# A decoder step on one core: the sample tokens' expert layer computed in the prologue, between the pieces of token tile 0's mixer

## The chip, the cores and the metric

One core of one Trainium2 chip runs the kernel. The metric is the device time in microseconds (us), lower is better. Most executions of a kernel agree within 0.3%.

## The reference

One layer of a hybrid decoder runs on 1024 prompt tokens and on 8 sample tokens, width 1024, in float32. Each token goes through a mixer (retention and dilated attention side by side) and then through PEER, a layer of product-key experts:

```python
qh = (xb @ w_pq).reshape(128, 8, 2, 64)             # 8 heads, two half queries
sc = einsum('thcq,hckq->thck', qh, sub_keys)        # 2 x 128 key scores a head
s1, i1 = top_k(sc[:, :, 0], 16); s2, i2 = top_k(sc[:, :, 1], 16)
# the best 16 of the 16 x 16 sums give 16 of the 16384 experts
g = softmax(top_s)
a = gelu(einsum('thkd,td->thk', peer_u[eidx], xb))
y = einsum('thk,thkd->td', g * a, peer_v[eidx])     # then x = x + gt2 * y
```

So each token reads 8 x 16 = 128 rows of `peer_u` and `peer_v`, 8 KB for the pair.

## The kernel before

Three blocks follow each other. `condition` makes the modulation rows. `decode` runs the sample's mixer and leaves its key scores in `sc_s`, its normed rows in the DRAM tensor `h2` and its mixed rows in `x_mid`. `layer`, from 262 us on, runs the prompt in T = 8 token tiles of 128. This document is about `layer`.

**The expert loop.** For each tile and head (N = 64 pairs, `n`) and each of 8 groups of two slots (`q`), POOL gathers one row of `uv` (u and v joined, 8 KB) for each of the 128 tokens: one indirect DMA of 1 MB a slot, into a ring of 8 buffers (`RING`). DVE takes the dot product with h2 (L1627), ACT makes Gelu, multiplies by the gate and scales the v half (L1107 to L1114), PE transposes and sums it in PSUM (`psA`, L1339) and then frees the two buffers (`s_free`), on which POOL's next two gathers wait. DVE chooses the experts of `n + 2` in the same groups (`choose`, parts 1 to 7).

**The mixer of each tile** is cut into pieces: on each engine a generator `front()` yields a due time and `Pace` runs the pieces between the loop's groups. Tile 0's pieces are all due at -1, so all of them run before the loop, in the order in which they are written: this is the prologue. Its order on PE: turn x, seven projections of four chunks (`product`, L1138), retention and attention of eight heads, turn of the mixed rows, output projection (2 products, w_out), turn of h2, queries (2 products, w_pq), turn of the queries; then `peer_scores` for the first three `n`. A projection's product writes one of two halves of `psS`, which DVE or ACT must have read before the next but one starts. DVE's evictions stand at `mark_read(t, j)`, its masking of the retention scores at L1443, the addition to x at L1544, the norm behind it at L1547 to L1554; ACT's square root of that variance is L1070.

**SP's queue** loads constants, then weight chunks of 512 KB into NB = 4 buffers `w`, each when PE has used the chunk four before it (`s_wu`), and the rows and stores of each tile.

**The sample's expert layer** has 8 tokens, whose 8 x 128 slots are turned: one gather a token, 128 experts on the partitions. Before, DVE chooses in the groups of n = N - 2; the choice goes to DRAM and comes back transposed by 8 small DMAs (16 experts x 8 tokens each) into `expT_f`, the gates the same way into `gateT`; POOL gathers behind the last prompt gather; DVE takes the dots against `h2b` (h2's row of each token, spread over 128 partitions and loaded by SP into `kTva`, free since the last tile's attention); ACT makes Gelu, DVE multiplies by the gate into one column of `coef`, and PE sums `coef` times v in `psS` (L1355). Two DVE operations and a store of y_sample end the kernel.

## Time and profile before

| | us |
|---|---|
| median of three runs | 3507.4 (3506.52 to 3515.91) |
| the profiled execution | 3499.32 |
| its span | 3497.5 |
| `layer` starts | 262.8 |
| first prompt gather, last prompt gather | 418.8, 3447.6 |
| DVE, ACT, PE busy, share of the span | 64%, 58%, 72% |

A busy share is a mean over the prologue, the loop and the tail, whose limits differ. In a timeline row stand the start in us, the length, the engine and the line, the operation, what it writes and reads, and the number of merged instructions (x16). In a windows row stand the stretch, its length, busy time and instructions of PE, PEld, DVE, ACT and POOL, the granted TensorE clock, the DMA share and GB/s. PE's float32 matmuls are recorded twice each: a 512-column product of one token is four records.

### The profile page before, as it was taken

What the parts mean: (1) busy time and instruction counts of PE and PEld (TensorE: products, weight loads), DVE (VectorE), ACT (ScalarE), POOL (GpSimd) and SP (SyncE); (2) the same over time, 40 slices, a digit from 0 to 9 for tenths busy, and PEclk for the clock granted to TensorE, in tenths of its full rate; (3) what the DMA queues carried; (4) which work ended last, traced back from release to release, by engine and by line L of the source; (5) the groups of instructions that cost most, each with busy time, mean ns of one, the idle gap of its engine ahead of it and who ended that gap; (6) DMA issues with size and microseconds to landing.
All of it is one profiled execution on the core that took longest, in us unless ns stands there. A gap on an engine that the chain in (4) does not pass through costs nothing.

```text
span 3497.5 us, 35906 instructions
## 1 busy us (share of the span) xinstructions
PE 2510.3 (72%) x12243; PEld 1758.0 (50%) x12243; DVE 2250.2 (64%) x5362; ACT 2037.0 (58%) x3417; POOL 1193.1 (34%) x1054
## 2 busy tenths in 40 slices
PE   8878587778767677688776776787776866565555
PEld 2224245445554565555654664555654655555553
DVE  0132366656676776666867876666976876776774
ACT  0101157655594776665766875665866766665663
POOL 0000023333342443333333433433333333444443
PEclk9988698889988888899787888899887888766777
DMA  8746599999999999999999999999999999999997
GB/s 311 260 152 203 196 373 381 392 374 414 414 401 396 390 394 413 406 415 415 408 413 406 387 393 413 405 415 416 411 406 406 384 396 403 421 420 413 414 419 316
DMA packets 272759, 1326.03 MB, mean 379 GB/s; under 512 B 36544, under 2 KB 37040, under 8 KB 139200
## 3 DMA queue, kind: packets, MB, share of 16 engines
q0 software_dynamic: 149072, 1083.68, 75.9%
q1 hardware_dynamic: 123504, 240.05, 19.0%
q8 instruction: 97, 1.59, 0.2%
q14 instruction: 86, 0.70, 0.0%
HBM read 1309.55 MB, written 14.09 MB: 378 GB/s over the span
## 4 chain that ended last, share of the span: by engine, by line
DMA 35%; PE 23%; ACT 16%; DVE 11%; issue 3%; POOL 3%; POOLq 0%; DVEq 0%; PEldq 0%; ACTq 0%
DMA pr_ring<-uv,pr_expert 25%; PE pairA L1339 11%; PE pairS L1138 9%; ACT pr_ring L1114 8%; DVE pr_ring L1627 6%; DMA sb_w<-w_out 4%; DMA sb_w<-w_pq 4%; POOL pr_ring L936 3%; ACT pr_act_h L1110 2%; ACT L1107 2%; PE bank L1138 2%; DMA sb_w<-w_in 1%; ACT L1060 1%; ACT pr_act_h L1107 1%; ACT pr_sp L1060 1%
## 5 line engine op out<-in xcount | busy, mean ns | idle before, releaser
L936 POOL DMA_INDIRECT pr_ring<-uv,pr_expert x1024 | 1170.0, 1143 | 2011.8 <-PE pairA L1339 1684.4
L1339 PE MATMUL pairA<-sb_ident,pr_ring 128*128 128x128 f32 x8192 | 1267.7, 322 | 758.1 <-ACT pr_ring L1114 742.0
L1627 DVE CUSTOM_DVE_ANT_0 pr_ring<-pr_ring,pr_h 128x1024 f32<-128x1024 f32 x1024 | 1241.8, 1224 | 645.8 <-DMA pr_ring<-uv,pr_expert 634.3
L1339 PEld LDWEIGHTS pairA<-sb_ident,pr_ring 128*128 128x128 f32 x8192 | 1142.6, 168 | 963.8 <-ACT pr_ring L1114 884.0
L1114 ACT ACTIVATE pr_ring<-pr_ring,pr_act_h 128x1024 f32<-128x1024 f32 x1024 | 1120.1, 1141 | 16.7
L1107 ACT ACTIVATE pr_act_h<-pr_dot 128x2 f32<-128x2 f32 x512 | 103.9, 203 | 891.0 <-DVE pr_dot L1627 889.5
L1138 PE MATMUL pairS<-sb_w,pr_hT 128*128 128x512 f32 x816 | 416.4, 647 | 74.8 <-DMA sb_w<-w_pq 51.8
L1138 PEld LDWEIGHTS pairS<-sb_w,pr_hT 128*128 128x128 f32 x816 | 158.3, 208 | 247.4 <-issue 145.9
L1110 ACT ACTIVATE pr_act_h<-pr_act_h,pr_gate_h 128x1 f32<-128x1 f32 x1024 | 245.9, 287 | 16.8
L1138 PE MATMUL pairS<-sb_w,pr_turned 128*128 128x512 f32 x256 | 140.0, 689 | 52.4 <-DMA sb_w<-w_out 49.6
L1107 ACT ACT_TABLE_LOAD x130 | 166.8, 1283 | 11.5 <-DVE pr_dot L1627 9.3
L1138 PE MATMUL bank<-sb_w,pr_sp 128*128 128x512 f32 x336 | 157.9, 593 | 0.0
L1138 PEld LDWEIGHTS pairS<-sb_w,pr_turned 128*128 128x128 f32 x256 | 52.3, 219 | 118.8 <-DMA sb_w<-w_out 66.3
L1138 PEld LDWEIGHTS bank<-sb_w,pr_sp 128*128 128x128 f32 x336 | 64.0, 191 | 80.8 <-issue 80.8
L1262 PE MATMUL pairS<-pr_kTva,pr_turned 64*128 64x512 f32 (+3 forms) x192 | 86.9, 564 | 13.4 <-DVE pr_st L1454 13.4
L164 PE MATMUL pairT<-ad_w,ad_cT 128*9 128x512 f32 x192 | 87.1, 608 | 10.0 <-DMA ad_w<-w_ada 10.0
L1627 DVE DVE_READ_ACCUMULATOR2_ANT pr_dot<- 128x1 f32 x1024 | 84.7, 83 | 0.0
L1093 ACT ACT_TABLE_LOAD x64 | 82.1, 1283 | 1.1
L1277 PEld LDWEIGHTS bank<-pr_kTva,pr_pt 128*128 128x128 f32 x504 | 78.1, 235 | 5.4 <-issue 2.1
L1277 PE MATMUL bank<-pr_kTva,pr_pt 128*128 128x65 f32 x504 | 78.4, 311 | 0.5 <-DVE pr_pt L1462 0.5
L1562 DVE MAX8 pr_top<-pr_work 128x8 f32<-128x128 f32 (+2 forms) x195 | 65.9, 338 | 4.6
L1544 DVE TENSOR_TENSOR pr_qk<-pairS,pr_rows 128x512 f32<-128x512 f32 x16 | 11.1, 691 | 85.5 <-PEq L1147 85.3
(304 smaller groups left out, 2040.0 us busy)
## 6 DMA issues: line engine op xcount, KB each, us to landing
sb_w<-w_in SPq DMA_DIRECT2D x140, 512.0 KB, 10.8
sb_w<-w_out SPq DMA_DIRECT2D x64, 512.0 KB, 11.7
sb_w<-w_pq SPq DMA_DIRECT2D x64, 512.0 KB, 11.5
ad_w<-w_ada SPq DMA_DIRECT2D x12, 2048.0 KB, 8.1
pr_ring<-uv,pr_expert POOLq DMA_INDIRECT x1024, 11.0
sb_wd<-w_in SPq DMA_DIRECT2D x7, 2048.0 KB, 9.1
pr_rows<-h SPq DMA_DIRECT2D x10, 512.0 KB, 6.7
de_kv<-k_sel SPq DMA_DIRECT2D x4, 1024.0 KB, 12.1
```

The lines of the kernel that those rows point to most:

```text
L164: last = pe.matmul(ps[c % 2][0:NC9, :], cT[:, k, :], w[c % WBUF][:, k, :], start=(k == 0), stop=(k == KT - 1))
L936: pool.indirect_dma_start(ring[r][:], None, a["uv"], bass.IndirectOffsetOnAxis(ap=index, axis=0)).then_inc(s_g[r], 16)
L1060: act.activation(sp[h % 2][:, 0:keys_of(t)], sp[h % 2][:, 0:keys_of(t)], ACT.Exp, bias=nmax[:, h:h + 1]).then_inc(s_P, 1)
L1093: act.activation(gate_h[n % 2][:], delta[n % 2][:], ACT.Exp, accum_out=gsum[n % 2][:, 0:1]).then_inc(s_ge, 1)
L1107: act.activation(act_h[:, c], dot[:, c], ACT.Gelu).then_inc(s_gelu, 1)
L1110: last = act.activation(act_h[:, s:s + 1], act_h[:, s:s + 1], ACT.Identity, scale=gate_h[u][:, s:s + 1])
L1114: last = act.activation(ring[s % RING][:, D:2 * D], ring[s % RING][:, D:2 * D], ACT.Identity, scale=act_h[:, s:s + 1])
L1138: last = pe.matmul(out, lhs[:, k, :], w[i % NB][:, j, :], start=(k == 0), stop=(k == KT - 1))
L1262: last = pe.matmul(psS[:, c], aqT[e, h // 2, :], kT[e, h // 2, c], start=True, stop=True)
L1277: last = pe.matmul(out, pt[:, k * P:(k + 1) * P], va[:, k, h * VA:(h + 1) * VA], start=(k == 0), stop=(k == t))
L1339: last = pe.matmul(psA[:, k * P:(k + 1) * P], ring[s % RING][:, D + k * P:D + (k + 1) * P], ident[:], start=(h == 0 and s == 0 and k % 4 = ...
L1627: last = dve.tensor_tensor_reduce(ring[r][:, 0:D], ring[r][:, 0:D], h2[t % 2][:], 1.0, 0.0, ALU.mult, ALU.add, dot[:, s:s + 1])
```

## The change

The sample's expert layer moves in front of the loop. ACT's queue starts with the loads of `h2b` and of the two small rows. DVE chooses after it has normed tile 0's x and before the first eviction. POOL, not SP, stores the choice and loads it transposed, and gathers four tokens, then four more into the same four buffers when PE has summed the first. The other four ring buffers hold `h2b`. DVE's dots, ACT's Gelus, DVE's coefficients and PE's sums stand in two halves between the pieces of tile 0. The sum lies in `psA`, which DVE reads behind the first choice of a prompt head. PE waits for that read before the loop. SP stores y_sample in tile 1's turn. The diff, cut:

```diff
-gt2s, xmid_s, y_s = x[0:B, :], sp[0][0:B, :], sp[1][0:B, :]
+gt2s, xmid_s = h2[1][0:B, :], xmid[0:B, :]
+HALF = B // 2
+h2b = [ring[HALF + b // 2][:, b % 2 * D:b % 2 * D + D] for b in range(B)]
...
             store_y(t - 2)
+        if t == 1:
+            spq.wait_ge(s_outs, 1)
+            spq.dma_start(a["y_sample"], xmid_s).then_inc(s_ys, 16)
+            spq.wait_ge(s_ys, 16)
         if t >= 1:
...
-    spq.wait_ge(s_q, 2 * T)
-    spq.wait_ge(s_TA, 5 * T)
+    store_y(T - 1)
     spq.wait_ge(s_owv, 16 * T)
-    spq.dma_start(gt2s, a["gt2_sample"]).then_inc(s_ws, 16)
-    spq.dma_start(xmid_s, a["x_mid"][T * P:T * P + B, :]).then_inc(s_ws, 16)
-    for b in range(B):
-        row = a["h2"][T * P + b:T * P + b + 1, :].to_broadcast([P, D])
-        spq.dma_start(h2b[:, b, :], row).then_inc(s_h2b, 16)
-    for n, (src, name) in enumerate(((expert_s, "expert_s"), (gate_s, "gate_s"))):
-        spq.wait_ge(s_gts, n + 1)
-        spq.dma_start(a[name].rearrange("h b k -> (h b) k"), src[:]).then_inc(s_xs, 16)
-    spq.wait_ge(s_xs, 32)
-    for dst, name in ((expT_f, "expert_s"), (gateT, "gate_s")):
-        for h in range(HP):
-            spq.dma_start(dst[h * TOPK:(h + 1) * TOPK, :], a[name][h].rearrange("b k -> k b"),
-                          allow_slow_non_contiguous=True).then_inc(s_xl, 16)
-    store_y(T - 1)
-    spq.wait_ge(s_out, T + 1)
-    spq.dma_start(a["y_sample"], y_s).then_inc(s_ys, 16)
     spq.wait_ge(s_owk, 16 * T)
...
     pool.memset(gretT[:], 1.0).then_inc(s_init, 1)
+    def store(n, src, name):
+        pool.wait_ge(s_gts, n + 1)
+        pool.dma_start(a[name].rearrange("h b k -> (h b) k"), src[:]).then_inc(s_xs, 16)
+    def place(n, dst, name):
+        pool.wait_ge(s_xs, 16 * n + 16)
+        for h in range(HP):
+            pool.dma_start(dst[h * TOPK:(h + 1) * TOPK, :], a[name][h].rearrange("b k -> k b"),
+                           allow_slow_non_contiguous=True).then_inc(s_xl, 16)
+    store(0, expert_s, "expert_s")
+    place(0, expT_f, "expert_s")
+    store(1, gate_s, "gate_s")
+    pool.wait_ge(s_xl, 16 * HP)
+    pool.tensor_copy(expT[:], expT_f[:]).then_inc(s_sxT, 1)
+    pool.wait_ge(s_sxT, 1)
+    for b in range(B):
+        if b == HALF:
+            place(1, gateT, "gate_s")
+        if b >= HALF:
+            pool.wait_ge(s_ysum, b - HALF + 1)
+        pool.indirect_dma_start(ring[b % HALF][:], None, a["uv"],
+                                bass.IndirectOffsetOnAxis(ap=expT[:, b:b + 1], axis=0)).then_inc(s_gs[b % HALF], 16)
+    pool.wait_ge(s_ysum, B)
     for n in range(N):
...
-    pool.wait_ge(s_xl, 32 * HP)
-    pool.tensor_copy(expT[:], expT_f[:]).then_inc(s_sxT, 1)
-    pool.wait_ge(s_sxT, 1)
-    for b in range(B):
-        if b % GRP == 0:
-            pool.wait_ge(s_free, N * GROUPS - RING // GRP + b // GRP + 1)
-        gather(b, expT[:, b:b + 1])
 @block.scalar
 def _(act):
+    for b in range(B):
+        row = a["h2"][T * P + b:T * P + b + 1, :].to_broadcast([P, D])
+        act.dma_start(h2b[b], row).then_inc(s_h2b, 16)
+    act.dma_start(gt2s, a["gt2_sample"]).then_inc(s_ws, 16)
+    act.dma_start(xmid_s, a["x_mid"][T * P:T * P + B, :]).then_inc(s_ws, 16)
     def front():
...
+            def sample_gelus(first):
+                for b in range(first, first + HALF):
+                    act.wait_ge(s_dots, b + 1)
+                    act.activation(act_h[:, b:b + 1], dot[:, b:b + 1], ACT.Gelu).then_inc(s_gelus, 1)
...
             if own(t):
+                if t == 0:
+                    act.wait_ge(s_tops, 1)
+                    act.activation(gate_s[:], delta_s[:], ACT.Exp, accum_out=gsum_s[:, 0:1]).then_inc(s_ges, 1)
                 yield mark_read(t, 0)
...
                 turned_rqk()
+            if t == 0:
+                sample_gelus(0)
             yield mark(t, 5)
...
             act.activation(std, var, ACT.Sqrt).then_inc(s_std, 1)
+            if t == 0:
+                sample_gelus(HALF)
             yield mark(t, 34)
...
             late = NPROJ if own(t) else 0
+            if t == 0:
+                sample_values(0)
             yield mark(t, 23)
...
+    def sample_values(first):
+        for b in range(first, first + HALF):
+            pe.wait_ge(s_dgs, b + 1)
+            for half in range(2):
+                last = pe.matmul(psA[0:B, half * 512:half * 512 + 512], coef[:, b, :],
+                                 ring[b % HALF][:, D + half * 512:D + half * 512 + 512],
+                                 start=(b == 0), stop=(b == B - 1), skip_group_check=True)
+            last.then_inc(s_ysum, 1)
...
         peer_scores(n)
+        if n == 0:
+            sample_values(HALF)
+    pe.wait_ge(s_outs, 1)
     for n in range(N):
...
-    for b in range(B):
-        pe.wait_ge(s_dgs, b + 1)
-        for half in range(2):
-            last = pe.matmul(psS[0:B, half * 512:half * 512 + 512], coef[:, b, :],
-                             ring[b][:, D + half * 512:D + half * 512 + 512],
-                             start=(b == 0), stop=(b == B - 1), skip_group_check=True)
-    last.then_inc(s_ysum, 1)
...
                     step(dve.tensor_scalar(mask[:], mask[:], 0.0, None, ALU.is_gt))
+                    for part in range(PARTS):
+                        choose(part, ROWS_S, sc_s, delta_s, expert_s)
+                    dve.sem_inc(s_tops, 1)
+                    dve.sem_inc(s_gts, 1)
                 for j in range(2):
...
                     dve.tensor_copy(qk[:, j * HW:(j + 1) * HW], psS[:, j * HW:(j + 1) * HW]).then_inc(s_evD, 1)
+                    if t == 0 and j == 0:
+                        dve.wait_ge(s_ges, 1)
+                        step(dve.reciprocal(gsum_s[:, 1:2], gsum_s[:, 0:1]))
+                        dve.tensor_scalar(gate_s[:], gate_s[:], gsum_s[:, 1:2], None, ALU.mult).then_inc(s_gts, 1)
                 dve.wait_ge(s_evD, 4 * EV[t] + 2)
...
                 weigh_rows(kw, psS[:, 512:1024], wend).then_inc(s_evD, 1)
+                if t == 0:
+                    sample_dots(0)
             else:
...
                               mask[:].unsqueeze(1).to_broadcast([P, H, P]), ALU.mult).then_inc(s_sT, 1)
+            if t == 0:
+                sample_coefs(0)
...
+            if t == 0:
+                sample_dots(HALF)
             for j in range(2):
...
             dve.tensor_scalar(var, ss, 1.0 / D, EPS, ALU.mult, ALU.add).then_inc(s_var, 1)
+            if t == 0:
+                sample_coefs(HALF)
             yield mark(t, 32)
...
+    def sample_dots(first):
+        dve.wait_ge(s_h2b, 16 * B)
+        for b in range(first, first + HALF):
+            r = b % HALF
+            dve.wait_ge(s_gs[r], 16 * (b // HALF) + 16)
+            dve.tensor_tensor_reduce(ring[r][:, 0:D], ring[r][:, 0:D], h2b[b], 1.0, 0.0, ALU.mult, ALU.add,
+                                     dot[:, b:b + 1]).then_inc(s_dots, 1)
+    def sample_coefs(first):
+        dve.wait_ge(s_xl, 32 * HP)
+        for b in range(first, first + HALF):
+            dve.wait_ge(s_gelus, b + 1)
+            dve.tensor_scalar(coef[:, b, b:b + 1], act_h[:, b:b + 1], gateT[:, b:b + 1], None, ALU.mult)\
+               .then_inc(s_dgs, 1)
...
+    step(dve.memset(coef[:], 0.0))
...
-    step(dve.memset(coef[:], 0.0))
...
+            dve.wait_ge(s_ysum, B)
+            dve.wait_ge(s_ws, 32)
+            step(dve.tensor_tensor(gt2s, psA[0:B, :], gt2s, ALU.mult))
+            dve.tensor_tensor(xmid_s, gt2s, xmid_s, ALU.add).then_inc(s_outs, 1)
...
-            if n == N - 2:
-                choose(q, ROWS_S, sc_s, delta_s, expert_s)
-                if q == GROUPS - 1:
-                    dve.sem_inc(s_tops, 1)
-                    dve.sem_inc(s_gts, 1)
-            if n == N - 1 and q == 4:
-                dve.wait_ge(s_ges, 1)
-                step(dve.reciprocal(gsum_s[:, 1:2], gsum_s[:, 0:1]))
-                dve.tensor_scalar(gate_s[:], gate_s[:], gsum_s[:, 1:2], None, ALU.mult).then_inc(s_gts, 1)
...
-    for b in range(B + 1):
-        if b < B:
-            dve.wait_ge(s_g[b], N * (TOPK // RING) * 16 + 16)
-            if b == 0:
-                dve.wait_ge(s_h2b, 16 * B)
-            dve.tensor_tensor_reduce(ring[b][:, 0:D], ring[b][:, 0:D], h2b[:, b, :], 1.0, 0.0,
-                                     ALU.mult, ALU.add, dot[:, b:b + 1]).then_inc(s_dot, 1)
-        if b == 0:
-            dve.wait_ge(s_xl, 32 * HP)
-        if b >= 1:
-            c = b - 1
-            dve.wait_ge(s_gelu, N * GROUPS + c + 1)
-            dve.tensor_scalar(coef[:, c, c:c + 1], act_h[:, c:c + 1], gateT[:, c:c + 1], None, ALU.mult)\
-               .then_inc(s_dgs, 1)
-    dve.wait_ge(s_ws, 32)
-    dve.wait_ge(s_ysum, 1)
-    step(dve.tensor_tensor(y_s, psS[0:B, :], gt2s, ALU.mult))
-    dve.tensor_tensor(y_s, y_s, xmid_s, ALU.add).then_inc(s_out, 1)
```

## Rows read from the trace of the kernel before

**Rows 1.** Windows view of the late loop; hardware queue in 3135 to 3185 us.

```profile
3200.00:3400.00 200.00, 118.58 (x648) 104.80 (x648) 145.83 (x358) 128.80 (x224) 98.16 (x80) 0.74 1.01 417
...
q1 hardware_dynamic: 1472, 5.31, 26.8%
```

**Rows 2.** Timeline of the last 30 us: start, length, engine, line, operation.

```profile
3469.08 0.36 SPq L861 DMA_DIRECT2D y_prompt<-pr_xmid  x1
...
3471.52 3.58 PE L1355 MATMUL pairS<-pr_ring,pr_coef 128*8 128x512 f32 x4 [3.81 <-DVE pr_coef L1677]
...
3479.08 1.88 PE L1355 MATMUL pairS<-pr_ring,pr_coef 128*8 128x512 f32 x4 [1.02 <-DVE pr_coef L1677]
...
3492.71 1.21 DVE L1681 TENSOR_TENSOR pr_sp<-pairS,sb_x 8x1024 f32<-8x1024 f32 x1 [3.40 <-PE pairS L1355]
...
3495.19 0.29 SPq L927 DMA_DIRECT2D y_sample<-pr_sp  x1
```

**Rows 3.** DMA issues of 260 to 430 us: count, size, us to landing.

```profile
x_mid<-pr_qk SPq DMA_DIRECT2D x1, 512.0 KB, 5.5
```

**Rows 4.** Timeline of SP late in the loop: the broadcasts of h2.

```profile
3141.04 4.30 SPq L916 DMA_DIRECT2D pr_kTva<-h  x8
```

**Rows 5.** Groups of POOL before 262 us: its dearest direct DMA.

```profile
L331 POOL DMA_DIRECT2D proj_s<-de_proj x1 | 0.8, 802 | 51.5 <-ACT de_proj L358 51.5
```

**Rows 6.** Timeline of the prologue's first part.

```profile
264.33 0.20 ACT L967 ACTIVATE pr_st<-pr_st 128x1 f32<-128x1 f32 x1 [1.97 <-DVE pr_st L1407]
...
264.76 2.14 DVE L1412 TENSOR_SCALAR sb_x<-sb_x,pr_st 128x1024 f32<-128x1024 f32 x1
...
272.75 0.20 DVE L1415 RECIPROCAL pr_qst<-pr_wend 128x8 f32<-128x8 f32 x1 [5.85 <-DMA pr_gretT<-g_ret_rows]
...
288.17 7.11 PE L1138 MATMUL pairS<-sb_w,pr_hT 128*128 128x512 f32 x16 [0.30 <-PE pairS L1138]
```

**Rows 7.** Windows view: the attention's heads, the first choice of a prompt head.

```profile
340.00:354.00 14.00, 11.39 (x36) 7.92 (x36) 6.59 (x30) 4.05 (x9) 0.00 (x0) 0.50 0.23 75
407.17:418.39 11.22, 1.86 (x4) 0.80 (x4) 9.77 (x37) 1.67 (x2) 0.00 (x0) 0.55 0.00 1
```

**Rows 8.** DMA queues, packets, MB, share: 455 to 540 us, then 280 to 326.

```profile
q0 software_dynamic: 2618, 18.97, 56.0%
...
q1 hardware_dynamic: 7113, 13.72, 43.2%
...
q1 hardware_dynamic: 6696, 12.90, 86.3%
```

**Rows 9.** Timeline of DVE at the masking; in brackets the idle time before it.

```profile
328.99 1.23 DVE L1443 TENSOR_TENSOR pr_pt<-pairS,pr_mask 128x1024 f32<-128x1024 f32 x1 [25.48 <-PE pairS L1238]
```

**Rows 10.** Timeline from the attention's end to the output projection.

```profile
353.02 0.69 PE L1277 MATMUL pairT<-pr_kTva,pr_pt 128*128 128x65 f32 x2 [0.45 <-DVE pr_pt L1462]
...
355.13 1.97 PE L1151 MATMUL pairT<-sb_ident,sb_x 128*128 128x128 f32 x8 [1.42 <-DVE sb_x L1527]
...
359.36 16.99 PE L1138 MATMUL pairS<-sb_w,pr_turned 128*128 128x512 f32 x32 [2.26 <-ACT pr_turned L1065]
...
368.93 0.69 DVE L1544 TENSOR_TENSOR pr_qk<-pairS,pr_rows 128x512 f32<-128x512 f32 x1 [13.86 <-PEq L1147]
```

**Rows 11.** Timeline of the loop's start.

```profile
420.17 0.97 POOL L936 DMA_INDIRECT pr_ring<-uv,pr_expert  x1 [0.30 <-issue]
...
430.29 1.23 DVE L1627 CUSTOM_DVE_ANT_0 pr_ring<-pr_ring,pr_h 128x1024 f32<-128x1024 f32 x1
...
436.99 1.28 ACT L967 ACT_TABLE_LOAD   x1
...
438.29 0.20 ACT L967 ACTIVATE pr_st<-pr_st 128x1 f32<-128x1 f32 x1
...
438.72 0.75 DVE L1412 TENSOR_SCALAR sb_x<-sb_x,pr_st 128x1024 f32<-128x1024 f32 x1
...
440.98 1.59 POOL L936 DMA_INDIRECT pr_ring<-uv,pr_expert  x1 [12.39 <-PE pairA L1339]
```

11 lines of the change are left out of this document (4 added, 7 removed).

## The prediction

> **What bounds the kernel now.** I read four things in this order: the busy table by stretches of the main loop, the timeline of the last 50 us, the timeline of the prologue (262 to 441 us), and the DMA queues in stretches with and without gathers.
>
> From 441 us to 3460 us the kernel gathers one megabyte per expert slot. A late stretch of 200 us shows a DMA share of 1.01 and 417 GB/s, with 80 gathers issued [rows 1]. So the loop's length is bytes over some 417 GB/s. Work of an engine inside it costs nothing while the DMA engines stay full. Bytes taken out of it shorten it, and a later start moves it whole. The two ends are different. In the tail, nothing follows the last sum but a short chain of dependent steps [rows 2]. In the prologue PE is the chain: projection, attention, output projection, queries; DVE and ACT have long holes in it, and the DMA engines are partly free.
>
> **What is removed.** The tail first. The prompt's last sum, turned and added to x_mid, ends in the store of y_prompt issued at 3469.08 [rows 2]. All of this stays. The store of y_sample is issued at 3495.19, and the span ends at 3497.5, 2.3 us later. With the sample gone, y_prompt's store is the end. The 32 KB store took 2.3 us; 512 KB add 1.2 us at 417 GB/s; with some allowance 4.2 us, so the span would end at 3473.3: **24.2 us less**. Bounds: 3.5 us for the store (24.9 less), or 5.5 us, as a store of this size took in the prologue [rows 3] (22.9 less).
>
> Then the loop. Eight broadcasts of h2 (8 x 512 KB = 4.19 MB) and two 32 KB rows are issued from 3140 us into full DMA engines [rows 4]. At 415 GB/s they are 10.3 us. The queue's own share agrees: in the 50 us around them the hardware queue held 26.8% of the DMA engines for 5.31 MB [rows 1], 13.4 us; 4.26 of these MB are 10.8 us. I take **10.3 us less**, bounds 10.0 and 10.8. The sample's choice on DVE (11 us in pieces) and its Exp on ACT leave a stretch in which DMA is full: worth nothing there. Gains: 34.5 us.
>
> **What is added in the prologue, in order.** All of it lies ahead of the first prompt gather, and every microsecond by which the chain is longer moves the whole loop.
>
> *Ten DMA issues at the head of ACT.* No row shows ACT issuing. On SP eight such broadcasts take 4.30 us, 0.54 each [rows 4]; POOL's dearest direct one took 0.80 [rows 5]. Ten at 0.54 are 5.4 us, so ACT's first Sqrt, at 264.33 before [rows 6], comes at 268.2: 3.9 us late, and DVE's normalisation of x, the turn, hT and the first product wait for it. One thing comes back: that normalisation took 2.14 us beside POOL's large memsets [rows 6] and 0.75 us in tile 1 [rows 11]; after 268 the memsets are over, so 1.4 us less. **+2.5 us**, bounds 2.0 and 5.1 (ten at 0.8).
>
> The Trainium skill ("DMA: Bandwidth & Descriptors", Issuing engines are not separate DMA queues) says that DMAs started from several engines interleave on the same 16 DMA engines, and that this saves only sequencer time. It would leave my sum as it is, for I count h2's 4.19 MB as traffic anyway, but it speaks against the placing: ACT's sequencer time is what the chain lacks here.
>
> *The choice on DVE.* It stands behind the constants, which landed at 272.75 [rows 6]. Sharing with h2's 4.19 MB may make that 275.7. The choice of a prompt head fills the 11.2 us from 407.17, DVE busy for 9.8 of them [rows 7]; with 64 rows the free sizes are the same, and I count 11. The end is 287.6, then the first eviction (0.7 us). PE needs that bank for its third product, before at 288.17 [rows 6], now at 290.7. So it just fits: **0**, up to 3 us if the constants wait for all of h2. Exp and the two small DVE steps fit before the second eviction.
>
> *Storing, placing, gathering four.* POOL was idle there. Store (land at about 290.5), eight transposed loads at 0.8 each (297, land at 300), the gate's store, a cast, four indirect gathers 1.27 us apart (0.97 and a hole of 0.30) [rows 11]: the gathers run from about 302 to 322. They move 4.19 MB beside the stream of w_in, which keeps PE fed through only four buffers. Without gathers this stream moved 12.90 MB in 46 us, 280 GB/s, at 86% of the DMA engines; with gathers beside it, in tile 1, 13.72 MB in 85 us, 161 GB/s, while gathers got 18.97 MB, 223 GB/s [rows 8]. At 223 GB/s four gathers last 18.8 us, and the stream loses 18.8 x (1 - 161/280) = 8.0 us. By conservation: 4.19 MB are 10.1 us of full DMA, and 14% of some 24 us were free, 3.3 us: 6.8 lost. I take **+7 us**, bounds 3 (they slip mostly behind the stream) and 10.1.
>
> *Dots, gelus and coefficients of the first half.* DVE had 25.48 us idle before the masking at 328.99 [rows 9]; four dots at 1.23 fit once the gathers have landed at about 322. Gelus on ACT and the four coefficients behind the masking lie in holes too. **0** while everything up to the gathers ends by 337 (the masking's new time).
>
> *PE's sums of the first half.* They stand behind the attention, which ends at 353.02 + 0.69 = 353.7, ahead of the turn of the mixed rows at 355.13 [rows 10]. One token was four records, 3.58 us when PE had just stood idle and 1.88 later [rows 2]; sixteen are 7.5 us at the higher clock. The attention ran at a granted clock of 0.50, the lower of the two levels [rows 7], so this stretch starts there; the output projection's first product, from 359.36 to its eviction at 368.93, took 9.6, 2.2 us more than a warm one (7.11 and 0.3 of hand-over) [rows 6, 10]. So 9.7 us, to 363.4: the turn is 8.3 us late. PE is then warm: the turn 0.9 and the product 2.2 shorter. **+5.2 us**, bounds 4 and 8.3 (the clock falls again while ACT copies).
>
> *The second four gathers* follow each sum, at about 358 to 364. DMA engines are then mostly free of weights until the projection's second half. They land by 372, dots done by 373.5, when the first eviction is due (368.93 + 5.2). **+1.5 us** for w_out behind them, bounds 0 and 10.1 (all of their bytes in PE's way).
>
> *Gelus of the second half* stand between ACT's Sqrt of x_mid's variance and DVE's reciprocal of it, because DVE's coefficients ahead of that reciprocal wait for them. A table load of 1.28 [rows 11], four Gelus at 0.20, as any ACT operation on one column [rows 11], with their hand-overs, one coefficient of about the same: **+2.4 us**. In the trace the Sqrt follows its table load at 436.99 at once, at 438.29 [rows 11]. The Trainium skill ("ScalarE: Activation LUTs", What ACT_TABLE_LOAD costs) gives a drain of 1.38 us beside the load, 2.66 us a switch; by it the term would be 3.8 and the net 12.0 us in place of 13.4. The trace shows no such hole here and decides.
>
> *PE's second sums* stand behind the first scores, while DVE chooses for 11 us: hidden, by about 2 us. *The sample's output*, two DVE operations at 1.21 us [rows 2], stands ahead of the second choice, and the first dots at 430.29 followed that choice without a pause; the ninth gather, at 440.98, waits for their group [rows 11]. **+2.5 us**. SP's early store of y_sample and its wait delay only loads that are due much later: 0.
>
> Losses: 2.5 + 7 + 5.2 + 1.5 + 2.4 + 2.5 = 21.1. Net: 34.5 - 21.1 = **13.4 us faster**. The profiled execution took 3499.32 (span 3497.5), so it becomes 3485.9. The median of the runs is 3507.4, 8.1 us above it; moved by the same amount it is **3494**, 0.38% less. About 10.5 us (0.3%) is what can be told from no change.
>
> **Rivals.**
> *The prologue gives it back (no change).* Here both sets of gathers stand fully in PE's way: 10.1 and 10.1 in place of 7 and 1.5, and PE's clock falls again (8.3 for 5.2). Losses 32.8, net 1.7 faster: 3506. For it speaks the rate of 161 GB/s beside gathers [rows 8] and the four buffers; against it, that the second set falls before the chunks of w_out's second half. The Trainium skill ("DMA: Bandwidth & Descriptors", SWDGE vs HWDGE vs iDMA) has each DMA engine take turns between the two kinds of queue; the 161 and 223 GB/s of [rows 8] agree.
>
> *It is nearly free (more gain).* The gathers fill only free DMA time (3 and 0), PE costs 4, the output 1.0 because the DMA engines still work off the first eight gathers, ACT 2.0: losses 12.4, net 22.1 faster: 3485. Against it: the measured sharing.
>
> *POOL's transposed loads are the chain (slower).* Each fetches 128 single elements; call one c. The gate's placing ends at about 302.5 + 16c; the first coefficients are due at 339, so it costs from c = 2.3 and has eaten the gain at 3.1. At c = 4 it ends at 366.5, 27.5 us late, and the net is 14 us slower: 3521. SP issued like ones in about half a microsecond, POOL's dearest direct DMA cost 0.80 [rows 5]: little for it.
>
> **How the numbers follow.** Chances: the forecast (8 to 20 us faster) 0.52, the prologue gives it back (8 faster to 5 slower) 0.27, nearly free (over 20 faster) 0.13, POOL's loads or another late hand-over (slower) 0.08. Faster by over 10.5 us: nearly all but a fifth of the first case, and the third, 0.54; same 0.38, slower 0.08. The bounds of the unknown costs reach from 24 us faster to 8 slower; the range keeps 25 faster to 1 slower, 3482 to 3508.
>
> **What the profile would show.** The span's end about 4 us behind y_prompt's store; no broadcast of h2 after 3100; ACT's first Sqrt at 268; the first gather of the sample near 302; chunks of w_in landing in 8 to 9 us in place of 4.6 while it lasts; the turn of the mixed rows at about 373; the ninth prompt gather at 462 in place of 440.98. The prediction is wrong if that last number is not 21 us later, if gathers land so late that DVE holds the masking, or if the loop's length from there does not shrink by 10 us.

## The result: 7 us faster, where 13.4 were forecast

| | us |
|---|---|
| before, median of 20 runs | 3510.35 (3502.56 to 3520.07) |
| changed kernel, median of 20 runs | 3503.38 (3489.66 to 3515.11) |
| ratio, 95% interval | 0.998 (0.997 to 0.9989) |
| profiled execution, its span | 3508.39, 3506.6 |

The change makes the kernel faster by 7 us (interval 4 to 10.5). Timed again on another chip it gave 3502.76 against 3507.82, a ratio of 0.9988 (0.9971 to 1.0004), an interval that just holds no change. The forecast of 3494 had the sign and nearly twice the size.

The profiled execution of the changed kernel is 9 us longer than that of before, while the medians say the opposite. Two profiles can't be subtracted at their ends: from the ninth gather on, the first forty head pairs took between 1946 and 1957 us in the thirteen profiles of this study, though none of the kernels changes the main work of these pairs. So I compare stages, each from its own start. For the prologue this is SP's first load of `layer` (262.5 here, 262.8 before, 256.5 to 262.9 in the kernels below, for the block ahead of it varies too).

**The end of the kernel**, in the timeline of the changed kernel:

```profile
3502.23 1.23 DVE L1720 TENSOR_TENSOR pr_xmid<-pairA,pr_xmid 128x1024 f32<-128x1024 f32 x1 [1.26 <-PE pairA L1385]
3503.48 0.34 SPq L866 DMA_DIRECT2D y_prompt<-pr_xmid  x1
```

The span ends at 3506.6, 3.1 us behind this store of 512 KB. Before, the end lay 28.4 us behind it [rows 2]. The tail gives 25.3 us; 24.2 were forecast.

**The prologue**, PE in the timeline of the changed kernel (start, length; in brackets the idle time before the row and what ended it):

```profile
274.25 9.08 PE L1158 MATMUL pairS<-sb_w,pr_hT 128*128 128x512 f32 x16 [2.99 <-ACT pr_hT L986]
283.81 7.13 PE L1158 MATMUL pairS<-sb_w,pr_hT 128*128 128x512 f32 x16 [0.49 <-DMA sb_w<-w_in]
294.94 8.83 PE L1158 MATMUL pairS<-sb_w,pr_hT 128*128 128x512 f32 x16 [3.99 <-DVE pr_qk L1454]
...
317.06 3.75 PE L1158 MATMUL pairS<-sb_w,pr_hT 128*128 128x512 f32 x4 [4.66 <-DMA sb_w<-w_in]
323.49 8.33 PE L1158 MATMUL pairS<-sb_w,pr_hT 128*128 128x512 f32 x12 [2.68 <-DMA sb_w<-w_in]
...
376.09 9.25 PE L1343 MATMUL pairA<-pr_ring,pr_coef 128*8 128x512 f32 x16
385.27 1.09 PE L1171 MATMUL pairT<-sb_ident,sb_x 128*128 128x128 f32 x8
388.63 7.13 PE L1158 MATMUL pairS<-sb_w,pr_turned 128*128 128x512 f32 x16 [2.27 <-ACT pr_turned L1090]
398.18 1.98 PE L1158 MATMUL pairS<-sb_w,pr_turned 128*128 128x512 f32 x4 [2.41 <-DMA sb_w<-w_out]
```

The third product, at 288.17 before [rows 6], begins at 294.94: PE stood idle for 3.99 us, and DVE's first eviction (L1454) released it. The product then took 8.83 us in place of 7.13. The fifth waited 4.66 and 2.68 us for w_in, and its parts are slow again: 3.75 us for four records that take 1.98 elsewhere. PE's sums at 376.09 took 9.25 us, and the product behind them is a warm 7.13.

DVE in the same timeline shows why the eviction was late:

```profile
282.78 0.20 DVE L1442 RECIPROCAL pr_qst<-pr_wend 128x8 f32<-128x8 f32 x1 [13.55 <-DMA pr_gretT<-g_ret_rows]
...
283.48 0.29 DVE L1601 MAX8 pr_top<-sb_sc_s 64x8 f32<-64x128 f32 x1
...
293.78 0.17 DVE L1634 SCALAR_TENSOR_TENSOR pr_expert_s<-pr_pick 64x16 f32<-64x16 f32 x1
294.19 0.69 DVE L1454 COPY pr_qk<-pairS 128x512 f32<-128x512 f32 x1 [0.24 <-DVE pr_expert_s L1634]
```

The choice takes 10.5 us, as forecast (11). But it stands behind the constants, and these landed at 282.78, not at 275.7: 10.0 us later than before [rows 6], 10.3 counted from the layer's start. h2's 4.19 MB at 415 GB/s are 10.1 us.

The windows view shows the rest (length; busy time of PE, PEld, DVE, ACT, POOL; granted clock, DMA share, GB/s). The changed kernel, and then before in the first two stretches:

```profile
294.00:298.00 4.00, 3.06 (x4) 1.31 (x5) 3.71 (x6) 1.59 (x3) 2.20 (x5) 0.66 0.13 46
298.00:303.00 5.00, 5.00 (x12) 2.24 (x11) 0.49 (x2) 0.22 (x1) 3.16 (x6) 0.93 0.54 134
303.00:324.00 21.00, 13.21 (x31) 5.49 (x30) 8.47 (x14) 1.63 (x5) 9.19 (x13) 0.80 1.02 373
324.00:334.00 10.00, 9.69 (x17) 3.73 (x16) 0.00 (x0) 0.60 (x1) 0.00 (x0) 0.73 0.60 178
```

```profile
294.00:298.00 4.00, 3.69 (x9) 1.46 (x9) 2.49 (x5) 0.00 (x0) 0.00 (x0) 1.00 0.91 323
298.00:303.00 5.00, 4.85 (x13) 1.91 (x12) 0.63 (x2) 0.00 (x0) 0.00 (x0) 1.00 0.93 297
```

While PE stood at the choice it freed no weight buffer, so the stream of w_in all but stopped: a DMA share of 0.13, then 0.54, where it was 0.91 and 0.93. Behind it come the four gathers and fill the DMA engines (1.02). Then PE runs at a granted clock of 0.73, between the two levels of 1.2 and 2.4 GHz (0.50 and 1.00), after two stalls, and the share falls to 0.60. The DMA engines are idle before and behind the gathers and full only with them.

The queues and POOL during and ahead of the gathers, in the changed kernel (the DMA view of 303 to 324 us, then POOL's timeline):

```profile
q0 software_dynamic: 855, 4.20, 51.8%
q1 hardware_dynamic: 1881, 3.63, 50.2%
...
sb_w<-w_in SPq DMA_DIRECT2D x6, 512.0 KB, 12.8
```

```profile
296.36 4.24 POOL L941 DMA_DIRECT2D pr_expT_f<-expert_s  x8 [1.40 <-DMA expert_s<-pr_expert_s]
...
303.94 1.04 POOL L955 DMA_INDIRECT pr_ring<-uv,pr_expT  x1 [0.28 <-POOL pr_expT L948]
...
449.32 0.94 POOL L928 DMA_INDIRECT pr_ring<-uv,pr_expert  x1 [62.77 <-DVE pr_expert L1645]
...
473.36 1.73 POOL L928 DMA_INDIRECT pr_ring<-uv,pr_expert  x1 [13.36 <-PE pairA L1374]
```

A chunk of w_in landed 12.8 us after its issue. The ninth prompt gather, at 440.98 before [rows 11], is at 473.36.

I use the following table for all kernels. It is worked out from such rows; each number is us from SP's first load of `layer`, in one profile. "Constants" is the landing of the last of them, "fourth" is the start of PE's fourth product, "va read" ACT's read of the last input projection, "evict" DVE's second addition to x, "ninth" the ninth prompt gather. Three profiles have the changed kernel's prologue: its own, that of its second timing, and that of the last experiment, whose edit begins only at n = 40.

```
                             constants  fourth  va read  mask   evict  ninth
before                            10.0    32.8     63.8   66.2  113.7  178.2
changed                           20.3    41.6     86.4   88.8  142.9  210.9
  its second timing               19.7    41.0     85.3   87.7  141.6  210.4
  choice repeated at n >= 40      19.8    41.2     81.7   84.1  137.1  205.6
choice early                      20.1    36.2     80.1   82.5  136.9  204.7
  timed                           20.1    36.5     80.9   83.3  136.6  203.9
h2 behind the constants           10.4    41.3     82.9   85.3  140.1  208.6
first gathers left out            20.3    41.6     72.7   75.1  129.6  197.0
PE kept busy                      20.1    39.7     84.0   86.4  139.2  208.2
first rearrangement               10.0    34.9     65.9   68.3  116.6  186.6
second rearrangement               9.9    34.3     66.5   68.9  116.5  181.3
  its gathers beside w_in          9.7    32.7     75.2   77.6  125.9  192.0
```

The three rows of the changed prologue show how far one profile can be trusted: up to the fourth product they agree within 0.6 us, and behind it they lie up to 5.3 us apart.

The ninth gather is 32.7 us later, where 21.1 were forecast. Tail and prologue together (25.3 - 32.7) would make the kernel 7.4 us slower. It is 7.0 faster by the medians, so the loop must have become some 14 us shorter, where 10.3 were forecast. The same sum over the second timing and the four other timed kernels below that lack the loop's loads (medians against the kernel before, each with the ninth gather of its own profile) gives 9 to 13 us, so the loop's share is known to a few us only. Two losses surely had the wrong size; the experiments take them apart.

### The profile page after: what moved, and what is told of

Read it like the earlier page. It is cut to its first block, busy times and chain, and to the rows that moved or that the text cites. A ratio compares the mean times of both kernels' runs of the same rounds, so it can differ in the third digit from the quotient of the medians.

```text
span 3506.6 us, 35904 instructions
## 1 busy us (share of the span) xinstructions
PE 2512.6 (72%) x12243; PEld 1761.8 (50%) x12243; DVE 2247.2 (64%) x5362; ACT 2039.0 (58%) x3419; POOL 1208.5 (34%) x1072
## 3 DMA queue, kind: packets, MB, share of 16 engines
q10 hardware_dynamic: 1184, 4.26, 0.3%
## 4 chain that ended last, share of the span: by engine, by line
DMA 36%; PE 23%; ACT 16%; DVE 11%; POOL 3%; issue 3%; SPq 0%; POOLq 0%; ACTq 0%; DVEq 0%; PEldq 0%
DMA pr_ring<-uv,pr_expert 25%; PE pairA L1374 11%; ACT pr_ring L1141 8%; PE pairS L1158 8%; DVE pr_ring L1692 5%; DMA sb_w<-w_out 4%; DMA sb_w<-w_pq 4%; POOL pr_ring L928 3%; DMA sb_w<-w_in 2%; ACT pr_act_h L1137 2%; ACT L1134 2%; PE bank L1158 2%; ACT L1085 1%; ACT pr_act_h L1134 1%; ACT pr_sp L1085 1%
## 5 line engine op out<-in xcount | busy, mean ns | idle before, releaser
L1374 PE MATMUL pairA<-sb_ident,pr_ring 128*128 128x128 f32 x8192 | 1283.5, 324 | 746.3 <-ACT pr_ring L1141 729.4
L1374 PEld LDWEIGHTS pairA<-sb_ident,pr_ring 128*128 128x128 f32 x8192 | 1162.6, 170 | 952.3 <-ACT pr_ring L1141 848.5
L1158 PEld LDWEIGHTS bank<-sb_w,pr_sp 128*128 128x128 f32 x336 | 63.8, 190 | 80.6 <-issue 80.6
L1282 PE MATMUL pairS<-pr_kTva,pr_turned 64*128 64x512 f32 (+3 forms) x192 | 84.1, 547 | 13.2 <-DVE pr_st L1494 13.2
L1606 DVE MAX8 pr_top<-pr_work 128x8 f32<-128x128 f32 (+2 forms) x195 | 65.9, 338 | 4.6
L1502 DVE TENSOR_TENSOR pr_pt<-pairT,pr_count 128x128 f32<-128x128 f32 (+7 forms) x64 | 48.4, 757 | 30.8 <-PE pairT L1171 29.1
```

What stands on the lines that cost most here:

```text
L1158: last = pe.matmul(out, lhs[:, k, :], w[i % NB][:, j, :], start=(k == 0), stop=(k == KT - 1))
L1282: last = pe.matmul(psS[:, c], aqT[e, h // 2, :], kT[e, h // 2, c], start=True, stop=True)
L1374: last = pe.matmul(psA[:, k * P:(k + 1) * P], ring[s % RING][:, D + k * P:D + (k + 1) * P], ident[:], start=(h == 0 and s == 0 and k % 4 = ...
```

## The experiments

### Is the stall at the choice the place of the choice?

The choice moves ahead of the wait for the constants; only `iota`, which its sixth part reads, gets a semaphore of its own.

```diff
+    for part in range(PARTS):
+        if part == 5:
+            dve.wait_ge(s_iota, 16)
+        choose(part, ROWS_S, sc_s, delta_s, expert_s)
     dve.wait_ge(s_const, ...)
     step(dve.reciprocal(qst[:], wend[:]))
     ...
-    for part in range(PARTS):
-        choose(part, ROWS_S, sc_s, delta_s, expert_s)
```

> The changed kernel, with DVE's choice of the sample's experts ahead of the wait for the constants instead of behind it (it waits only for iota, before its fifth part). In the changed kernel the constants land at 282.78 us, the choice ends at 293.95, PE's third product starts at 294.94 after standing idle for 3.99 and takes 8.83 in place of 7.13. Theory (the placing behind late constants costs 4.0 us of stall and 1.7 us of clock): the choice runs from about 269 to 281, the third product starts at about 291.2 without a stall and takes 7.1, and the fourth starts some 5.5 us earlier, at 298.5 in place of 304.07. Rival (the loss comes from the weight stream behind h2's broadcasts, not from DVE): the third product still starts at 294 or later, for want of weights. The ninth prompt gather, at 473.36 in the changed kernel, comes at 468 by the theory and at 473 by the rival.

PE in the timeline of this kernel (`layer` starts at 256.5):

```profile
277.64 7.13 PE L1159 MATMUL pairS<-sb_w,pr_hT 128*128 128x512 f32 x16 [0.59 <-DMA sb_w<-w_in]
285.08 7.32 PE L1159 MATMUL pairS<-sb_w,pr_hT 128*128 128x512 f32 x16 [0.30 <-DMA sb_w<-w_in]
292.70 1.96 PE L1159 MATMUL pairS<-sb_w,pr_hT 128*128 128x512 f32 x4 [0.30 <-PE pairS L1159]
300.31 3.78 PE L1159 MATMUL pairS<-sb_w,pr_hT 128*128 128x512 f32 x4 [5.65 <-DMA sb_w<-w_in]
```

The stall and the slow third product are gone, the fourth product comes 5.4 us earlier and the ninth gather 6.2. The constants are as late as before this edit. From the fourth product to "va read" it still takes 43.9 us (44.8 in the changed kernel, 31.0 before). One run took 3491.64 us, beside 3504.96 for the kernel before.

Timed, to see whether these 6 us reach the end:

> The same kernel as the first experiment (the choice ahead of the constants), now timed against the kernel before. Theory (the time of the loop's start passes on to the end one to one): 6.2 us less than the change's -7.0, so 13 us faster than before, a ratio of 0.996. Rival (the loop gives back what the prologue gains, for its length is set by more than bytes): no more than 8 to 9 us faster, 0.9975.

It took 3499.26 us against 3507.96, ratio 0.9969 (0.9955 to 0.9983): 11 us faster by the ratio, 8.7 by the medians. The interval holds both theories. The gain at the fourth product is plain (36.2 and 36.5 beside 41.0 to 41.6 in three profiles of the changed prologue). At the ninth gather 204.7 and 203.9 stand beside 210.9, 210.4 and 205.6, so there it may be as little as 1 us; that it reaches the end isn't settled by this pair.

### Are the constants late because ACT's loads share the DMA engines?

The ten loads go from the head of ACT's queue to SP's, behind the constants and ahead of the loop over the tiles.

> The changed kernel, with the ten sample loads issued by SP behind the constants, in place of by ACT at its head. Theory: the constants land at about 273 as in the kernel before (282.78 in the changed one), because they no longer share with 4.19 MB; ACT's first Sqrt is at 264.3 again (268.04), the first product starts at 272 (274.25), the choice ends near 285 and DVE never holds PE, so the third product starts at 289 to 291 (294.94). Rival: h2's broadcasts now stand in SP's queue ahead of the first weight chunks, and what the constants gain PE loses waiting for the fifth chunk: the second product starts at 283 or later and the third at 292 or later. The ninth prompt gather comes at 467 by the theory, at 470 to 473 by the rival.

PE in the timeline (`layer` starts at 261.2):

```profile
270.36 8.68 PE L1157 MATMUL pairS<-sb_w,pr_hT 128*128 128x512 f32 x16 [2.99 <-ACT pr_hT L985]
284.75 10.01 PE L1157 MATMUL pairS<-sb_w,pr_hT 128*128 128x512 f32 x16 [5.71 <-DMA sb_w<-w_in]
```

The constants land at 10.4 us, as before the change, and the choice ends at 21.4. So it was h2's traffic that held them. But now w_in waits behind these 4.19 MB: PE idles for 5.71 us one product earlier, and the fourth product, at 41.3, gains only 0.3 us. Ahead of it the bytes cost about the same in either place. One run took 3506.99 us.

### What do the first four gathers cost?

POOL fills the four buffers with zeros in place of the first four gathers, so `y_sample` lacks four tokens. All else stays, POOL's 16 transposed loads too.

```diff
+            if b < HALF:
+                pool.memset(ring[b][:], 0.0).then_inc(s_fill, 1)
+                continue
             pool.indirect_dma_start(ring[b % HALF][:], None, a["uv"], ...)
```

> The changed kernel with the first four gathers of the sample left out (POOL fills those four buffers with zeros, so the sample's output lacks four tokens); stores, transposed loads, dots and sums stay. In the changed kernel the fourth product starts at 304.07 and the last input projection is read by ACT at 348.88, 44.8 us later, against 31.0 us in the kernel before (295.58 to 326.60): 13.8 us more. Theory (gathers beside the weight stream, and the clock that falls when PE waits for it): the stretch is back to about 31 us, the ninth prompt gather comes 13 to 14 us earlier, at 460. Rival (the 16 transposed loads of single elements are what clogs the DMA engines): the stretch stays above 38 us and the ninth gather comes after 466.

From the fourth product to "va read" takes 31.1 us, as before the change (31.0), and 44.8 with the gathers. The ninth gather comes 13.8 us earlier (one run: 3493.88 us). The gathers cost 13.8 us in that profile; the transposed loads cost nothing. In the other two profiles of the changed prologue the stretch is 44.4 and 40.5 us, so the same gathers cost 13.3 and 9.5 there.

### How much of it is PE's clock?

PE makes 24 idle transposes while it waits for the choice, and 32 and 16 where it waits for w_in.

```diff
+    for k in range({(2, 0): 24, (4, 0): 32, (4, 1): 16}.get((n, q), 0) if t == 0 else 0):
+        pe.transpose(psA[:, k % 8 * P:(k % 8 + 1) * P], ident[:], ident[:])
```

> The changed kernel with idle work on PE where it stalled in tile 0: 24, 32 and 16 transposes of the identity into psA ahead of the third product and of the first two quarters of the fifth (the stalls were 3.99, 4.66 and 2.68 us; the fillers take 0.13 us each at the higher clock). Nothing else changes; the fillers' result is never read. Theory (half of the loss beyond the bytes is TensorE's clock, which falls in each stall: 8.83 in place of 7.13 for the third product, 3.75 for a quarter of the fifth and 8.33 for its other three quarters in place of 1.8 and 5.3): the third product takes 7.1, the quarters 1.8 and 5.3, and the last input projection is read by ACT 3 to 6 us earlier than 348.88, the ninth prompt gather at 467 to 470. Rival (PE only waits for bytes, so a faster clock just waits longer): the products are short but start later, the last projection is read within 1.5 us of 348.9, the ninth gather at 472 to 474.

```profile
289.83 2.81 PE L1213 MATMUL pairA<-sb_ident 128*128 128x128 f32 x24
293.71 7.13 PE L1158 MATMUL pairS<-sb_w,pr_hT 128*128 128x512 f32 x16 [1.06 <-DVE pr_qk L1456]
...
317.19 1.98 PE L1158 MATMUL pairS<-sb_w,pr_hT 128*128 128x512 f32 x4 [0.76 <-DMA sb_w<-w_in]
323.51 6.05 PE L1158 MATMUL pairS<-sb_w,pr_hT 128*128 128x512 f32 x8 [4.34 <-DMA sb_w<-w_in]
```

The third product is at 7.13 us again, and the fourth comes 1.8 us earlier: that is the clock's share of the choice's 6.2 us. Behind the fourth product the stretch is 44.2 us in place of 44.8, no more than the profiles differ by. There PE, now fast, waits again for w_in (4.34 us): the bytes are the limit. One run took 3511.68 us.

### Would the gathers cost less behind the stream of w_in?

A rearranged version. The choice stands ahead of the constants. ACT issues h2's loads behind its last projection read, in place of the first Gelus, and POOL waits for that same read:

```diff
+    place(1, gateT, "gate_s")
+    pool.wait_ge(s_evA, 3)
     for b in range(B):
-        if b == HALF:
-            place(1, gateT, "gate_s")
```

Each half of dots, Gelus, coefficients and sums moves one gap later: the first sums stand behind the output projection, the last Gelus behind hT's copy and no longer beside DVE's norm.

> The same version with the sample's two output operations left on DVE between the first and second choice. Against the other version this has two DVE operations of 1.21 us on the path: 2.1 to 2.5 us more, ninth gather that much later. If it shows no difference, the loop's start was bound by the first gathers' landing and not by DVE.

3480.34 us, ratio 0.9909 (0.9884 to 0.9933). The last input projection is read at 65.9 us of the layer; 63.8 before the change.

The second rearrangement also takes the sample's output from DVE's path: ACT copies the sum out of PSUM, and DVE's two operations stand in a group of the loop.

> A version put together from the changed kernel's trace. Choice early as in the first experiment; h2's spreads issued by ACT behind the last input projection (DMA engines free there, ACT idle for 11 us); the first four gathers wait until the input projections are over; their dots stand behind the mixed rows, their Gelus behind ACT's copy of them, their coefficients behind the first addition to x, PE's first sums behind the output projection (PE idle there for some 6 us); the second dots, Gelus and coefficients stand behind h2, where DVE is idle for 24 us; ACT copies the sample's sum out of psA and DVE's two output operations move into the loop. Theory (in the prologue only what shares the DMA engines with a weight stream or stands between two pieces of PE's chain costs): the ninth prompt gather comes within 4 us of the 440.98 of the kernel before, and with 25 us less tail and 10 us less loop the whole is 30 to 36 us faster than before (0.9 to 1.0%), 23 to 29 us faster than the change. Rival (the eight gathers cost their 20 us of DMA wherever they stand in the prologue): ninth gather at 455 to 462, the whole 15 to 20 us faster than before.

3472.47 us, ratio 0.989 (0.9865 to 0.9915): about 36 us faster than the kernel before, the best version here. The ninth gather comes at 181.3, 3.1 us later than before. That is 5.3 us ahead of the first rearrangement. From the first to the ninth gather it takes 22.0 us in place of 24.2, which is the two DVE operations. Most of the rest is one product of the queries: 7.14 us here, at a granted clock of 1.00, and 9.79 there, at 0.72, behind an idle time of 3.48 and 3.69 us. The edit touches nothing ahead of that product, so this part is not its doing.

Now only the wait for `s_evA` is taken out of it:

> The second rearranged version, with one wait taken out: the first four gathers of the sample no longer wait for the end of the input projections, but start as soon as the choice has been placed, some 25 us after the layer's start, while w_in streams in. Everything else of that version stays (in it the ninth prompt gather comes at 181.3 us of the layer, the last input projection is read at 66.5). Theory (what cost 13.9 us in the change is the place of these gathers beside w_in's stream, whatever else stands around them): the last input projection is read at 77 to 80, the ninth prompt gather comes 9 to 13 us later, and the median is 3481 to 3486 against 3472.5. Rival (the stream suffered in the change because h2's broadcasts and the stall at the choice had already emptied the weight buffers; with the choice early and h2 loaded later, full buffers ride over four gathers): the ninth gather less than 6 us later, 3478 or less.

POOL's gathers and PE in the timeline (`layer` starts at 258.1):

```profile
291.63 1.05 POOL L957 DMA_INDIRECT pr_ring<-uv,pr_expT  x1 [0.30 <-issue]
...
303.47 3.09 PE L1163 MATMUL pairS<-sb_w,pr_hT 128*128 128x512 f32 x4 [3.63 <-DMA sb_w<-w_in]
309.51 7.82 PE L1163 MATMUL pairS<-sb_w,pr_hT 128*128 128x512 f32 x12 [2.96 <-DMA sb_w<-w_in]
```

The same two waits for w_in are back. "va read" comes 8.7 us later, the ninth gather 10.7, and the median is 3486.44 (ratio 0.9923, 0.9902 to 0.9943), 11.6 us more than with the wait, ratio against ratio. The ninth gather comes where the theory had it (9 to 13 us later), "va read" earlier than its 77 to 80. So the place beside w_in's stream costs. But the 8.7 can't be set against the 13.8: from the fourth product to "va read" it takes 42.5 us here, 31.0 in the kernel before and 32.2 with the wait, so in the measure of the 13.8 the gathers cost 10.4 to 11.5 us. (The fourth product came 1.6 us later in the version with the wait, ahead of anything that differs between the two.)

Does a stall ahead of the gathers make them dearer? The kernels with the early choice answer it: PE's idle time ahead of its third product is 0.30 and 0.82 us there, in place of 3.99, and the gathers still cost 12.9 and 13.4 us. What differs between dear and cheap gathers is what follows them. The timed early choice ahead of its gathers and in the 10 us behind their landing, then the last experiment's kernel behind its own:

```profile
279.50:288.50 9.00, 8.18 (x20) 3.52 (x19) 2.62 (x3) 0.00 (x0) 4.78 (x9) 1.00 0.82 263
308.30:318.30 10.00, 9.85 (x23) 4.36 (x23) 3.70 (x6) 1.63 (x5) 0.00 (x0) 0.73 0.64 209
```

```profile
320.50:330.50 10.00, 9.29 (x21) 3.45 (x20) 1.23 (x2) 0.60 (x1) 0.00 (x0) 0.94 0.94 302
```

A DMA share of 0.64 behind the gathers goes with a cost of 13.4 us, one of 0.94 with 9.5. The same window in the six other profiles with gathers beside w_in has 0.66, 0.69, 0.71 and 0.82 with costs of 13.3, 13.8, 13.2 and 12.9, and 0.72 and 0.86 with 11.5 and 10.6. So what comes on top of the bytes goes with idle time of the DMA engines behind the gathers. PE's granted clock there goes much the same way (0.61 and 0.73 in the dearest two, 0.94 and 1.00 in the cheapest two), and these profiles don't part the two. Why the same code gives 13.8 once and 9.5 another time stays open.

### What are h2's loads worth in the loop?

In the kernel before, each spread of h2 is loaded four times in place of once: 12.58 MB more. DVE's wait for `h2b` is raised to all four loads.

```diff
+    for rep in range(1, 4):
+        spq.wait_ge(s_h2b, 16 * B * rep)
+        for b in range(B):
+            row = a["h2"][T * P + b:T * P + b + 1, :].to_broadcast([P, D])
+            spq.dma_start(h2b[:, b, :], row).then_inc(s_h2b, 16)
```

> The kernel before, in which each of the eight spreads of h2 in the late loop is loaded four times, one set after the other: 12.58 MB more in the loop. Theory (the loop is bytes over 415 GB/s, so taking 4.19 MB out was worth 10.3 us): 30 us slower than before, 3538 to 3542 at a median of 3510 (ratio 1.0086). Rival (a broadcast that reads one row 128 times is cheaper or is partly hidden, so that the removed traffic was worth little): under 15 us slower.

3532.60 us, ratio 1.0064 (1.0042 to 1.0086): 24.5 us more by the medians, or 1.95 us/MB. At that rate the 4.19 MB would be 8.2 us. The profiles show where the time goes. A pair begins with every sixteenth prompt gather of POOL; so the time between such gathers is the length of a pair. The first gathers of n = 56 and n = 60, before and then in the changed kernel:

```profile
3113.43 1.81 POOL L936 DMA_INDIRECT pr_ring<-uv,pr_expert  x1 [0.78 <-PE pairA L1339]
...
3290.06 0.98 POOL L936 DMA_INDIRECT pr_ring<-uv,pr_expert  x1 [1.61 <-PE pairA L1339]
```

```profile
3160.83 1.75 POOL L928 DMA_INDIRECT pr_ring<-uv,pr_expert  x1 [0.85 <-PE pairA L1374]
...
3323.54 0.94 POOL L928 DMA_INDIRECT pr_ring<-uv,pr_expert  x1 [0.30 <-issue]
```

```
pairs 56 to 59    before 176.6    changed 162.7    h2 loaded four times 206.1
                  ten other profiles without these loads  162.0 to 163.7
pair 62           before  40.0    changed  40.6
```

The four pairs hold SP's broadcasts [rows 4], and they got **13.9 us** shorter. By them the first 4.26 MB cost 3.3 us/MB, the next 12.58 another 29.5 us, 2.3 us/MB. But the pairs just ahead went the other way: 48 to 55 took 350.2 us before and 351.7 to 360.2 in the rest. Over pairs 48 to 59 together the kernel before took 526.8 us and the eleven profiles without the loads 514.3 to 522.3, which leaves only 4.5 to 12.5 us for the loads. So 13.9 is what four pairs of one profile show, and not yet the loop's gain.

### Or is part of it the choice, taken out of pair 62?

The changed kernel, with the sample's choice repeated in the groups of eight pairs. It uses the scratch of the prompt's choice, which runs in the same groups, so other rows (as many bytes) are gathered for these pairs and `y_prompt` comes out wrong.

```diff
+    if 40 <= n < 48:
+        choose(q, ROWS_S, sc_s, delta_s, expert_s)
```

> The changed kernel, with the sample's choice on DVE repeated in the groups of eight token-head pairs in the middle of the loop (n = 40 to 47), as it stood in one pair before the change; about 10 us of DVE work each, 80 us in all, whose results nobody reads. The main loop got some 14 us shorter, and the bytes of h2's broadcasts explain 8 to 10 of them. Theory (the rest is the choice: in a full loop it still delayed the sums that free the gathers' buffers): some 4 us for each repetition, 25 to 40 us longer than the change, 3528 to 3543. Rival (work of an engine costs nothing while DMA is full, as the prediction had it): within 5 us of the change, 3498 to 3508, and the rest of the 14 us stays open.

It took 3538.9 us, ratio 1.0078 (1.0055 to 1.01), 36 us more than the changed kernel on the same chip. Pairs 40 to 47 took 406.6 us, where the twelve other profiles have 375.4 to 379.3: 3.6 us for each added choice. So the rival's "costs nothing while DMA is full" is wrong for a second choice beside the prompt's own. But the theory falls as well: before, the sample's choice had pair 62 to itself, where no prompt head is chosen, and that pair was no longer with it (40.0) than without (40.6). It gave nothing of the loop's gain.

The changed kernel beside it:

> The changed kernel itself, timed again on the same chip as the repetition of the choice: some 7 us faster than before, a ratio of 0.997 to 0.999, by all theories.

3502.76 us, ratio 0.9988; its ninth gather is at 210.4 us of the layer and its pairs 56 to 59 take 163.2 us.

## Why the prediction had the sign right and the size wrong

Each term from the table and the rows above, one profile of each kernel, in us:

```
term                         forecast   measured   from
tail                            -24.2      -25.3   store to end, 28.4 to 3.1
loop, h2's bytes                -10.3      -13.9   pairs 56 to 59
ACT's ten issues                 +2.5       +2.6   first product 9.1 to 11.7
choice on DVE                     0         +6.2   fourth product, +8.8 less 2.6
first four gathers               +7        +13.8   fourth product to va read
hole before the masking           0          0     va read and mask, both 22.6 later
PE's sums + second gathers       +6.7       +6.7   mask to evict, 47.5 to 54.2
Gelus of the second half         +2.4       +2.1   evict to h2, 3.3 to 5.4
h2 to the first gather            -         -0.6   39.0 to 38.5
sample's output                  +2.5       +1.9   first to ninth gather
sum                             -13.4       -6.5   medians: -7.0
```

The losses were 11.6 us larger than forecast. By the same table the gains were 4.7 larger too, which hid part of it: that the kernel still came out faster owes something to luck.

**Right:** the tail, ACT's late Sqrt, and the chain behind the attention. ACT issued eight broadcasts in 4.56 us, 0.57 each (0.54 forecast), and its Sqrt came at 268.04 (268.2). POOL's transposed loads took 0.53 us each to issue, far from the 2.3 at which the slower rival begins. The second set of gathers hid as forecast, but for the idle 2.41 us at 398.18. For the Gelus the text weighed a drain of 1.38 us beside the table load. The Sqrt of the variance ended at 408.55, the load ran from 408.57 to 409.85, the first Gelu began at 409.87: no drain here, against what the Trainium skill ("ScalarE: Activation LUTs", What ACT_TABLE_LOAD costs) has.

**The step that failed first** is "The choice on DVE: 0", and in it the landing of the constants, "sharing with h2's 4.19 MB may make that 275.7". Both queues begin together, the constants are 1.4 MB in all, and the last of them landed when all of h2 had: 272.75 + 4.19 MB / 415 GB/s = 282.8, measured 282.78. The rate was in the text, for the loop's gain, and not used here. Even its bound was wrong: by its own steps (11.9 us from the constants to the choice's end, 0.7 for the eviction), "up to 3 us if the constants wait for all of h2" should have read 282.8 + 11.9 + 0.7 = 295.4 for the third product, 4.7 behind 290.7; it began at 294.94. Measured are 3.7 of new idle time, 1.7 for the slower product behind it, and 0.7 in and between the first two products. The first experiment shows that the order on DVE alone removes 5.4 of the 6.2 us. The Trainium skill ("DMA: Bandwidth & Descriptors", Issuing engines are not separate DMA queues) was applied to ACT's sequencer alone; its other half, that transfers of several issuers interleave on the same engines, is what happened to SP's constants, and the two placings of h2's loads agree with it.

**The second** is "First four gathers: +7", whose upper bound of 10.1 (all bytes at full DMA) lies below the 13.8. That bound supposed that the DMA engines stay full beside and behind the gathers. The stream of w_in did not keep them so: with four buffers it runs at most four chunks ahead of PE, and while PE waited for chunks that the gathers held up, it freed few buffers: SP issued a single chunk between 311.20 and 327.30 us. In the 10 us behind the gathers' landing the DMA share was 0.69, and 0.94 in the profile where they cost 9.5. The stall at the choice is not the reason, as the early choice shows (12.9 and 13.4 us without it). So these are two separate failures. Of the clock, 1.8 us were shown ahead of the fourth product and none clearly behind it.

**The rivals.** A gain of 7 us lies in the band of "the prologue gives it back", but two of its three causes did not come: the second gathers hid, and PE's clock did not fall behind the sums (a product of 7.13 us at 388.63). What filled the band was the choice, which that rival did not have. Its sum was wrong as well: with its own terms the losses are 2.5 + 10.1 + 8.3 + 10.1 + 2.4 + 2.5 = 35.9 and the kernel 1.4 us slower, not 32.8 and 1.7 faster.

**Not settled** is the loop, forecast at 10.3. Four pairs show 13.9, twelve pairs 4.5 to 12.5, the sums over the timed kernels 9 to 14, and the fourfold load 1.95 us/MB, or 8.2. The forecast lies inside, so this term can't be called wrong, nor can it be said that a burst of loads costs more than its bytes. The rows in [rows 1] have 13.4 us of queue share for 5.31 MB; from that I took 10.8 as a bound for h2's part.

## What to carry to other kernels

Before a bulk load is moved to the start of a stage, look for the small loads issued beside it and at what stands behind the last of them: here 4.19 MB made the last constant 10.3 us later. A weight stream with a few buffers is not a reservoir: a stall of its consumer left the DMA engines idle here, whether it came from another engine or from the bulk transfer itself, so bytes over bandwidth is no upper bound for what a bulk transfer costs beside such a stream. Put bulk traffic where the consumer doesn't stream (here during the attention, in a version which with an earlier choice and a shorter path on DVE was worth 36 us in place of 7). Profile the same code more than once before a difference of 5 us in a later stage is given a cause: three profiles of one prologue had the four gathers at 13.8, 13.3 and 9.5 us. And check what is taken out of a loop against a wider stretch than the passes that held it.

## What the runs showed of the hardware that I had not expected

- SP's ten constants (2 to 512 KB each) landed no sooner than ACT's bulk issued beside them: the last, 2 KB, 15.4 us after its issue, and 5.3 us in the second rearrangement, where the bulk comes later.
- A 512 KB store with nothing beside it let the span end 3.1 us after its issue, less than the 3.5 of my lower bound.
- After an idle time of 4.66 to 5.65 us four records of a product took 3.75 to 3.78 us in place of 1.98, twice as long, as at the lower of PE's two clock levels; transposes in the gap kept them at 1.88 to 1.98.
